# Second layer's modulation on TensorE instead of VectorE, a new hand-over into the down projection, and half of the down weights' low parts on VectorE

## The chip, the cores and the metric

The kernel runs on one core of a Trainium2 chip. The metric is the device time of one execution in microseconds; the time before is the median of three runs. TensorE's clock stands at one of two levels, 1.2 or 2.4 GHz; the profile gives the granted clock as a share of the full one.

## The reference

Two layers over 1024 latent tokens and 256 context tokens of width 1024: layer 0 mixes with a bidirectional RG-LRU, layer 1 with neighbourhood attention, and each is followed by a ConvFFN of width 2816. Each layer is modulated: six rows of 1024 values (shift, scale and gate, twice) come from the conditioning vector and a 1024 x 6144 matrix, once for the latent tokens (`c`) and once for the context tokens (`c_ctx`).

```python
mods = split(silu(c) @ mod_w[l] + mod_b[l], 6)
xl = xl + mods[2] * mixer(modulate(rmsnorm(xl, norm1_g[l]), mods[0], mods[1]))
zl = modulate(rmsnorm(xl, norm2_g[l]), mods[3], mods[4])
xl = xl + mods[5] * conv_ffn(zl, ffn_w_up[l], ffn_conv_w[l], ffn_conv_b[l], ffn_w_down[l])
def conv_ffn(z, w_up, conv_w, conv_b, w_down):
    u = dwconv(z @ w_up, conv_w, conv_b, FFN_CONV // 2)
    g, v = jnp.split(u, 2, axis=-1)
    return (jax.nn.silu(g) * v) @ w_down
```

The context stream needs only the first 16 of layer 1's 48 columns of 128 modulation values, the latent stream all 48.

## The kernel before, in words

All five engine programs are written out by hand: each engine runs its instructions in the order of the code, and semaphores tie them together. Products are made from split operands: a matrix is held as a high part (the value rounded for TensorE, an ACT copy) and a low part (value minus high part, a subtraction), and three matmuls (high x high, high x low, low x high) make one product.

The change lies in the first layer's ConvFFN. `up_first` makes the hidden rows, one pair of columns `i` after another (`KF` = 22 of them), in two rounds each. After the last one its tail still runs inside the next part: ACT's `mid_g`, `mid_v` and `silu`, VectorE's last sum `c21`, the taps `taps_g` and `taps_v`, and `gated`; then SP stores that last row to memory (`store`), and it comes back as the last tile of the next part's moving operand.

`down_first` is that next part. It works in `N` = 132 chunks in three blocks of 44 (blocks 0 and 1: 512 token columns each, block 2: 256). In a block there are four passes of 11 chunks; a chunk is 12 matmuls over two rows of the hidden matrix and two tiles of output. So 88 chunks have 512 columns and 44 have 256. For chunk n SP loads 256 KB of weights (`load_w`, allowed once chunk n - 7 is used, since there are seven pages), ACT makes the high part (`w_high`), and GpSimd, or in block 2 for every fourth chunk VectorE, the low part (`w_low`; `by_dve` decides). In the first pass of each block the moving operand is loaded and split too: `load_h` on SP, `high` on ACT, `low` on VectorE; tile pair x = 10 of block 0 holds the row that `gated` makes last. In ACT's program `high(0, 10)` stands at n = 4, behind `w_high` of chunk 11. In VectorE's program all the `low(0, x)` of block 0 stand ahead of its loop over n, and the `w_low` of chunk n + 7 stands in that loop at n.

Beside this the part makes the second layer's modulation. In 24 steps 1 MB each of `mod_w[1]` are loaded by GpSimd's queue (`load_mod`, two DMAs a step, two buffers). VectorE makes 32 column sums (`columns`, 8 instructions each, every one waiting for the one before), TensorE turns them two at a time (`turn`, 4 transposes behind chunk `TURN_AT`), and VectorE adds the turned columns up (`turned`). TensorE waits in `turn` for `mod_row`, GpSimd in `load_mod` for the sums of step q - 2. From chunk 89 on the next norm runs beside block 2 (`norm.sums`, `root`, `inverse`, `spread`, then `z`), which needs the modulation.

The first layer's modulation is made elsewhere, by `mod_step`: four matmuls with the two conditioning columns stationary, each writing its own 32 partitions of one PSUM bank, and `mod_turn` of four transposes.

Of the kernel before, what the change touches and what calls it, by code (L numbers as in the profile page):

```python
# [2792 lines left out]
def first_places(nc, m):  # L2793

    modring_at, ring_at, z_at, arena = m.at
    page = D * 4
    half = TOK // 2
    row = TOK * 4

    def at(name, place, shape, dt=F32):  # L2800
        return Plan(nc, place).put(name, shape, dt)

    m.f_H = [at(f"f_slotH{p}", ring_at + page * p, [P, BANK], F32R) for p in range(9)]
    m.f_L = [at(f"f_slotL{p}", ring_at + page * p + page // 2, [P, BANK], F32R) for p in range(9)]
# [5 lines left out]
    m.f_mod = [[m.modw.rearrange("p (k n) -> p k n", k=KD)[:, 4 * h:4 * h + 4, :] for h in range(2)],  # L2810
               [at(f"f_mod1{h}", ring_at + page * p, [P, 4, 2 * P]) for h, p in enumerate((5, 8))]]
# [24 lines left out]


def up_first(nc, m, norm, nxt):
# [408 lines left out]
    def vector(dve):  # L3247
# [125 lines left out]
        for i in range(HEAD, KF):  # L3373
# [29 lines left out]
            if more:  # L3403
                low(i + 1, S3)
            else:
                nxt.early_vector(dve)
# [16 lines left out]
def down_first(nc, m, norm, nxt):  # L3423
# [8 lines left out]
    mod_order, mod_row, mod_T, mod_copied = [sem("e_" + n) for n in ("mod_order", "mod_row", "mod_T", "mod_copied")]  # L3432
    part = Bag()
    down = m.t["ffn_w_down"][0].rearrange("(k p) n -> p k n", p=P)
    mod_w = m.t["mod_w"][1].rearrange("(k p) n -> p k n", p=P)
# [6 lines left out]
    MOD_STEPS = 3 * KD  # L3442
    WIDE = 2 * P
    CHAINS = [(q, s) for q in range(KD) for s in range(2)] + [(q, 0) for q in range(KD, MOD_STEPS)]
    TURNS = len(CHAINS) // 2
    PER_PASS = {1: 5, 2: 6, 3: 3, 4: 5, 5: 6, 6: 5}
    CHAIN_AT = [5, 8] + [NX * p + j * NX // n for p, n in PER_PASS.items() for j in range(n)]
    SUM_AT = {at: n for n, at in enumerate(CHAIN_AT)}
    LAST_OF = {q: n for n, (q, s) in enumerate(CHAINS)}
    LOAD_AT = {CHAIN_AT[LAST_OF[q - 2]] + 1: q for q in range(2, MOD_STEPS)}  # L3450
    TURN_AT = {CHAIN_AT[2 * n + 1] + 4: n for n in range(TURNS)}
    assert len(CHAIN_AT) == len(SUM_AT) == len(CHAINS) and len(LOAD_AT) == MOD_STEPS - 2 and len(TURN_AT) == TURNS
    VALUES_AT = max(TURN_AT) + 1
# [9 lines left out]
    def column_sum(n):  # L3463
        return m.zLraw[:, 2 * (n % 4):2 * (n % 4) + 2, BANK:BANK + P]

    def turned_at(n):
        return MISC + n % 2 * BANK
# [34 lines left out]
    def page_free(eng, p):  # L3502
# [3 lines left out]
        else:  # L3506
            eng.wait_ge(mod_row, len(CHAINS))
# [3 lines left out]
    def tiles_free(eng, b, x):  # L3511
# [8 lines left out]
        elif x < 2:  # L3520
            eng.wait_ge(mod_row, len(CHAINS))
# [23 lines left out]
    def load_mod(gp, q):  # L3545
        if q >= 2:
            gp.wait_ge(mod_row, [n for n, (step, s) in enumerate(CHAINS) if step == q - 2][-1] + 1)
        elif q == 0:
            gp.wait_ge(part.prev.g_conv, KF)
        else:  # L3550
            gp.wait_ge(part.prev.prod_done, part.prev.n_products)
        for h in range(2):
            gp.dma_start(m.f_mod[q % 2][h][:, :, :], mod_w[:, 4 * h:4 * h + 4, q * WIDE:(q + 1) * WIDE]).then_inc(mod_in[q % 2], 16)
# [14 lines left out]
    def sync(sp):  # L3568
# [11 lines left out]
        for n in range(PAGES, N):  # L3580
# [34 lines left out]
    def by_dve(n):  # L3615
        return n >= THREE and n % 4 == 1
# [39 lines left out]
    def scalar(act):  # L3656
        prev = part.prev
        for n in range(3, 5):
            w_high(act, n)
        for x in (2, 3):  # L3660
            high(act, 0, x)
        prev.mid_v(KF - 1)
        for n in range(5, 7):
            w_high(act, n)
        for x in (4, 5):
            high(act, 0, x)
        prev.silu(KF - 1)
        for x in range(6, NX - 1):
# [21 lines left out]
    def gpsimd(gp):  # L3690
# [19 lines left out]
    def tensor(pe):  # L3710
        def turn(n):
            pe.wait_ge(mod_row, 2 * n + 2)
            if n >= 2:
                pe.wait_ge(mod_copied, n - 1)
            for b in range(4):
                x = column_sum(2 * n + b // 2)[:, b % 2, :]
                ins = nc.tensor.transpose(ps[:, turned_at(n) + b * P:turned_at(n) + (b + 1) * P], x, m.ident[:, :])
# [3 lines left out]
        for n in range(N):  # L3721
# [40 lines left out]
    def vector(dve):  # L3762
        def turned(n):

            dve.wait_ge(mod_T, n + 1)
            q = CHAINS[2 * n][0]
            src = ps[:, turned_at(n):turned_at(n) + BANK]
            if n < KD:
                nc.vector.tensor_reduce(m.mod[:, 1, :, 2 * q:2 * q + 2], src.rearrange("p (s b x) -> p s b x", s=2, b=2), AX_X, ALU.add).then_inc(mod_copied, 1)
            else:  # L3770
                nc.vector.tensor_reduce(m.mod[:, 1, 0, 2 * q:2 * q + 4], src.rearrange("p (b x) -> p b x", b=4), AX_X, ALU.add).then_inc(mod_copied, 1)

        def columns(n):

            q, c = CHAINS[n]
            if n >= 4 and n % 2 == 0:
                turned(n // 2 - 2)
            dve.wait_ge(mod_in[q % 2], 32 * (q // 2 + 1))
            acc = column_sum(n)
            chain = Order(dve, mod_order, (KD - 1) * n)  # L3780

            def row(k):
                return m.f_mod[q % 2][k // 4][:, k % 4, :].rearrange("p (b n) -> p b n", b=2)

            chain(nc.vector.tensor_scalar(acc, row(0), m.ccol[:, 0, c:c + 1], None, ALU.mult))
            for k in range(1, KD):
                ins = nc.vector.scalar_tensor_tensor(out=acc, in0=row(k), scalar=m.ccol[:, k, c:c + 1], in1=acc, op0=ALU.mult, op1=ALU.add)
                if k < KD - 1:
                    chain(ins)
            ins.then_inc(mod_row, 1)  # L3790

        def mod_values():
            turned(TURNS - 2)
            turned(TURNS - 1)
            dve.wait_ge(mod_copied, TURNS)
            for c, n in enumerate((N_MOD, 2 * KD)):
                nc.vector.tensor_tensor(m.mod[:, 1, c, 0:n], m.mod[:, 1, c, 0:n], vcol(m, "mod_b1", 0, n), ALU.add).then_inc(mod_copied, 1)

        def mod_gains():
            dve.wait_ge(mod_copied, TURNS + 2)  # L3800
# [59 lines left out]
    part.mod_row, part.sums = mod_row, len(CHAINS)  # L3860
# [1110 lines left out]
```

## Time and profile before

| what | us |
|---|---|
| median of three runs | 2914.04 (2911.12 to 2914.94) |
| the profiled execution's own time | 2910.09 |
| its span | 2908.3 |
| down part of the first layer, first product to last | 1160.7 to 1561.0 of the span |
| TensorE busy in the span | 2800.8 (96%) |
| mean granted clock | 0.984 |

Times within the profile are counted from the start of the span. A matmul's record is longer than the distance to the next one, since matmuls overlap, so durations of work on TensorE are read from start to start. "Busy" is the union of the records. An idle time in brackets stands before the instruction, with what released it.

### The profile page before, as it was taken

Reading aid. Unit: us, or ns where it says so; the run is one execution under the profiler, and the core shown is the slowest. Engines: PE = TensorE matmul, PEld = TensorE weight load, DVE = VectorE, ACT = ScalarE, POOL = GpSimd, SP = SyncE. Lnnn points to the kernel's source line nnn. Section 1 sums busy time; section 2 is a strip of 40 time slices with the busy share of each in tenths; the row PEclk is TensorE's granted clock in tenths of the full one; section 3 lists DMA queues with packets and bytes.
Section 4 is the critical chain, followed back from the end, with each engine's and each line's share of the span. In section 5 each row is a group of like instructions: output and inputs, shape, how many; then the busy total and the mean of one; then the engine's idle time right before and its main releaser. Section 6 shows DMA issues by size and latency. Waiting matters only on the chain. (4 is left out here: it accounts for less than half of the span.)

```text
span 2908.3 us, 42045 instructions
## 1 busy us (share of the span) xinstructions
PE 2800.8 (96%) x16269; PEld 2408.3 (83%) x16269; DVE 1892.1 (65%) x2649; ACT 1300.7 (45%) x1881; POOL 821.3 (28%) x639
## 2 busy tenths in 40 slices
PE   8999999999999999888799999999999999999999
PEld 6888887879999999666688888888788788887888
DVE  7667666288888887899955035545638888885111
ACT  6676884164444333323144144444524544444331
POOL 3322230230000000655546343433414000005653
PEclk9999999999999999899899999999999999999999
DMA  9544334211222223756554343332433222227442
GB/s 338 147 120 116 112 89 183 96 33 64 72 71 71 71 71 105 257 175 206 189 192 134 111 142 88 95 88 80 128 124 102 87 87 78 82 68 259 157 132 73
DMA packets 349414, 355.90 MB, mean 122 GB/s; under 512 B 48275, under 2 KB 301554, under 8 KB 347168
## 3 DMA queue, kind: packets, MB, share of 16 engines
q1 hardware_dynamic: 333504, 298.86, 32.4%
q0 software_dynamic: 15680, 54.35, 5.9%
q8 instruction: 131, 2.15, 0.3%
q14 instruction: 67, 0.55, 0.1%
q10 hardware_dynamic: 32, 0.01, 0.0%
HBM read 284.02 MB, written 66.13 MB: 120 GB/s over the span
## 5 line engine op out<-in xcount | busy, mean ns | idle before, releaser
L3624 POOL TENSOR_TENSOR f_slotL<-f_slotS,f_slotH 128x512 fp32r<-128x512 f32 x121 | 167.8, 1404 | 590.3 <-ACT f_slotH L3601 589.9
L4662 POOL TENSOR_TENSOR slotL<-slotS,slotH 128x512 fp32r<-128x512 f32 x88 | 124.2, 1421 | 453.5 <-ACT slotH L4592 453.5
L3210 PE MATMUL ps<-zL,f_slotH 128*128 128x320 f32 x640 | 197.5, 310 | 1.4 <-DVE f_keptR L3268 1.4
L3210 PE MATMUL ps<-zH,f_slotH 128*128 128x320 f32 x640 | 198.1, 310 | 0.5 <-ACT f_snap L3066 0.5
L3210 PE MATMUL ps<-zH,f_slotL 128*128 128x320 f32 x640 | 198.1, 310 | 0.0
L2363 POOL TENSOR_SCALAR S<-S,rowstat 128x608 f32<-128x608 f32 (+1 forms) x63 | 136.0, 2159 | 199.4 <-DVE rowstat L2651 199.4
L3601 ACT ACTIVATE f_slotH<-f_slotS 128x512 fp32r<-128x512 f32 x132 | 81.8, 627 | 220.5 <-DMA f_slotS<-in_ffn_w_down_dram 220.4
L3210 PE MATMUL ps<-f_keptR,f_slotH 128*128 128x320 f32 x640 | 170.1, 310 | 0.0
L2564 ACT ACTIVATE S<-S,rowstat 128x640 f32<-128x640 f32 (+1 forms) x128 | 103.5, 809 | 144.1 <-DVE rowstat L2646 144.1
L4260 PE MATMUL ps<-zH,slotH 128*128 128x512 f32 x400 | 156.2, 391 | 1.2 <-DVE U L4357 1.2
L4260 PE MATMUL ps<-zL,slotH 128*128 128x512 f32 x400 | 156.2, 390 | 1.1 <-DVE slotL L4328 1.1
L4260 PE MATMUL ps<-zH,slotL 128*128 128x512 f32 x400 | 155.8, 390 | 0.0
L2646 DVE CUSTOM_DVE_ANT_0 S<-ps,bias 128x640 f32<-128x640 f32 (+1 forms) x128 | 98.1, 804 | 81.5 <-PE ps L2411 81.0
L776 PE MATMUL ps<-zH,wH 128*128 128x512 f32 (+1 forms) x408 | 145.7, 357 | 0.0
L776 PE MATMUL ps<-zL,wH 128*128 128x512 f32 (+1 forms) x408 | 144.6, 354 | 0.0
L776 PE MATMUL ps<-zH,wL 128*128 128x512 f32 (+1 forms) x408 | 144.6, 354 | 0.0
L4697 PE MATMUL ps<-zH,slotH 128*128 128x512 f32 (+1 forms) x360 | 133.3, 370 | 4.2 <-DVE res_last L4752 2.4
L4697 PE MATMUL ps<-zL,slotH 128*128 128x512 f32 (+1 forms) x360 | 132.4, 368 | 0.0
L4697 PE MATMUL ps<-zH,slotL 128*128 128x512 f32 (+1 forms) x360 | 132.4, 368 | 0.0
L3746 PE MATMUL ps<-zH,f_slotH 128*128 128x512 f32 (+1 forms) x320 | 125.7, 393 | 3.3 <-DVE zL L3612 2.5
L3746 PE MATMUL ps<-zL,f_slotH 128*128 128x512 f32 (+1 forms) x320 | 123.2, 385 | 0.0
L3746 PE MATMUL ps<-zH,f_slotL 128*128 128x512 f32 (+1 forms) x320 | 122.9, 384 | 0.0
(524 smaller groups left out, 8591.2 us busy)
## 6 DMA issues: line engine op xcount, KB each, us to landing
f_slotS<-in_ffn_w_down_dram SPq DMA_DIRECT2D x132, 256.0 KB, 3.3
slotS<-in_ffn_w_down_dram SPq DMA_DIRECT2D x88, 256.0 KB, 2.6
wraw<-in_ffn_w_up_dram SPq DMA_DIRECT2D x36, 512.0 KB, 4.0
modw<-in_mod_w_dram POOLq DMA_DIRECT2D x16, 1024.0 KB, 6.7
wraw<-in_na_w_in_dram SPq DMA_DIRECT2D x32, 512.0 KB, 4.1
bias<-scratch_bias SPq DMA_DIRECT2D x512, 32.0 KB, 1.8
f_slotS<-in_ffn_w_up_dram SPq DMA_DIRECT2D x60, 256.0 KB, 2.9
scratch_h<-f_V SPq DMA_DIRECT2D x22, 640.0 KB, 2.9
```

The source lines that it names most:

```text
L776: last = nc.tensor.matmul(ps[:, slot * SLOT + c:slot * SLOT + c + n], w(k), r(k)[:, c:c + n], start=(k == 0 and i == 0), stop=(k == K - 1 ...
L2363: nc.gpsimd.tensor_scalar(x, x, m.rowstat[:, g % 2, 5:6], None, ALU.mult).then_inc(scaled[1], 1)
L2564: nc.scalar.activation(s, s, ACT.Exp, scale=-1.0, bias=m.rowstat[:, g % 2, hd:hd + 1], accum_out=m.rowstat[:, g % 2, 2 + hd:3 + hd]).then_ ...
L2646: nc.vector.tensor_tensor_reduce(m.S[:, g % 2, hd, 0:n], ps[:, at:at + n], m.bias[:, s % 2, h, hd, 0:n], -1.0, 3.0e38, ALU.add, ALU.min, m ...
L3210: ins = nc.tensor.matmul(out_of(i, p, x), wt[:, w], z, start=(fresh and k == 0 and n == 0), stop=(k == 3 and n == 2), skip_group_check=True)
L3601: nc.scalar.activation(m.f_H[page(n)][:, :], m.f_S[page(n)][:, :], ACT.Copy).then_inc(d_high, 1)
L3624: ops.tensor_tensor(m.f_L[p][:, :], m.f_S[p][:, :], m.f_H[p][:, :].bitcast(F32), ALU.subtract).then_inc(low_dve if by_dve(n) else low_pool, 1)
L3746: ins = nc.tensor.matmul(out, wt, h, start=(x == 0 and kk == 0 and i == 0), stop=(x == NX - 1 and kk == 1 and i == 2), skip_group_check=True)
L4260: ins = nc.tensor.matmul(out, w, z, start=(fresh and k == 0 and n == 0), stop=(k == 3 and n == 2), skip_group_check=True)
L4662: nc.gpsimd.tensor_tensor(m.slotL[slot(n)][:, :], m.slotS[slot(n)][:, :], m.slotH[slot(n)][:, :].bitcast(F32), ALU.subtract).then_inc(d_lo ...
L4697: ins = nc.tensor.matmul(out, wt, h, start=(first and i == 0), stop=(last and i == 2), skip_group_check=True)
```

## The change

It does four things. (1) The modulation of layer 1 is made by TensorE, as in layer 0: 24 steps of four matmuls, step q behind chunk 7 + 3q, three groups of eight steps; each group is copied out by VectorE, turned by four transposes behind the second chunk after it, and added to the bias by VectorE. VectorE's 32 column sums, 16 reductions and TensorE's 16 turns go. (2) The 24 loads of 1 MB move from GpSimd's to SP's queue, in rows of 2048 values instead of 256. (3) The hand-over: in VectorE's program the first two `low` pairs stand behind the last round's `x12`, `c22` and `c12` instead of before them; the later `low`s stand between the taps; ACT's order changes likewise; VectorE clears one PSUM bank. (4) `by_dve` gives VectorE the low part of every second chunk from 7 on.

```diff
@@ up_first, vector, last column @@
-            else:
-                nxt.early_vector(dve)
             x12(i, 1)
             c22(i, 1)
 ...
                 low(i + 1, S4)
+            else:
+                nxt.early_vector(dve)
@@ down_first @@
+    GROUPS, STEPS = N_MOD * P // MODG, N_MOD * P // MODG * KD
+    STEP_AT = [7 + 3 * q for q in range(STEPS)]
+    GROUP_AT = [STEP_AT[KD * g + KD - 1] for g in range(GROUPS)]
@@ load_mod, now called by sync @@
+        if q >= 2:
+            sp.wait_ge(mod_used, q - 1)
 ...
+        g, k = divmod(q, KD)
+        src = mod_w[k][:, g * MODG:(g + 1) * MODG]
+        if q % 2 == 0:
+            sp.dma_start(m.modw[:, :], src).then_inc(mod_in[0], 16)
+            return
+        for h in range(2):
+            sp.dma_start(m.f_mod1[h][:, :], src[:, h * D:(h + 1) * D]).then_inc(mod_in[1], 16)
@@ sync, in the loop over n, behind load_w, store and residual @@
+            for q, at in enumerate([PAGES + 2, PAGES + 4] + [at + PAGES + 1 for at in STEP_AT[:STEPS - 2]]):
+                if n == at:
+                    load_mod(sp, q)
@@ by_dve @@
-        return n >= THREE and n % 4 == 1
+        return n >= PAGES and n % 2 == 1
@@ scalar @@
-        for n in range(3, 5):
-            w_high(act, n)
-        for x in (2, 3):
-            high(act, 0, x)
+        w_high(act, 3)
+        high(act, 0, 2)
+        w_high(act, 4)
+        high(act, 0, 3)
         prev.mid_v(KF - 1)
-        for n in range(5, 7):
-            w_high(act, n)
         for x in (4, 5):
             high(act, 0, x)
         prev.silu(KF - 1)
+        for n in (5, 6):
+            w_high(act, n)
@@ tensor @@
+        def mod_step_of(q):
+            g, k = divmod(q, KD)
+            pe.wait_ge(mod_in[q % 2], (16, 32)[q % 2] * (q // 2 + 1))
 ...
+            for j in range(4):
+                ins = nc.tensor.matmul(ps[32 * j:32 * j + 2, MACC:MACC + BANK], m.ccol[:, k, :], mod_rows(q, j), start=(k == 0), stop=(k == KD - 1))
+            ins.then_inc(mod_used, 1)
 ...
+            if n in STEP_AT:
+                mod_step_of(STEP_AT.index(n))
+            if n - 2 in GROUP_AT:
+                turn(GROUP_AT.index(n - 2))
@@ vector @@
-        for x in (2, 3):
-            low(dve, 0, x)
-        prev.c21(KF - 1, 1)
-        prev.taps_g(KF - 1)
-        prev.taps_v(KF - 1)
-        for x in (4, 5):
-            low(dve, 0, x)
-        prev.gated(KF - 1)
-        for x in range(6, NX - 1):
-            low(dve, 0, x)
-        low(dve, 0, NX - 1)
+        prev.c21(KF - 1, 1)
+        low(dve, 0, 2)
+        prev.taps_g(KF - 1)
+        low(dve, 0, 3)
+        low(dve, 0, 4)
+        prev.taps_v(KF - 1)
+        low(dve, 0, 5)
+        prev.gated(KF - 1)
+        dve.wait_ge(prev.c11_done, 2 * (KF - HEAD))
+        nc.vector.memset(ps[:, MACC:MACC + BANK], 0.0).then_inc(mod_zeroed, 1)
+        for x in range(6, NX):
+            low(dve, 0, x)
 ...
-            if n in SUM_AT:
-                columns(SUM_AT[n])
+            if n - 1 in GROUP_AT:
+                mod_row_of(GROUP_AT.index(n - 1))
+            if n - 3 in GROUP_AT:
+                mod_columns(GROUP_AT.index(n - 3))
```

## Rows read from the trace of the kernel before

**Rows 1.** Windows of the down part: length, busy (x instructions) by engine, clock, DMA.
```profile
1160.74:1191.36 30.62, 24.06 (x84) 18.88 (x85) 23.07 (x31) 16.67 (x27) 14.32 (x9) 0.83 0.71 248
1191.36:1204.96 13.60, 13.60 (x61) 11.26 (x60) 8.02 (x10) 2.94 (x5) 9.15 (x8) 1.00 1.03 372
1204.96:1488.65 283.69, 236.33 (x978) 190.81 (x976) 261.78 (x322) 74.42 (x131) 152.47 (x135) 0.92 0.57 190
1488.65:1561.00 72.35, 69.67 (x565) 67.83 (x563) 50.97 (x62) 41.20 (x73) 50.98 (x37) 1.00 0.66 217
```

**Rows 2.** Waits from 1160 to 1490: who for whom, total, times, longest.
```profile
PE ps L3717 <- DVE zLraw L3787: 47.4, 14, 4.9
POOL modw L3553 <- DVE zLraw L3787: 41.1, 10, 7.6
```

**Rows 3.** Groups by shape from 1160.74 to 1488.65: busy, mean ns, idle before.
```profile
L3624 POOL TENSOR_TENSOR f_slotL<-f_slotS,f_slotH 128x512 fp32r<-128x512 f32 x89 | 121.3, 1380 | 56.7 <-ACT f_slotH L3601 56.3
...
L3787 DVE SCALAR_TENSOR_TENSOR zLraw<-f_mod,ccol,zLraw 128x256 f32<-128x256 f32 x112 | 98.5, 879 | 4.0
L3787 DVE SCALAR_TENSOR_TENSOR zLraw<-modw,ccol,zLraw 128x256 f32<-128x256 f32 x112 | 95.8, 855 | 4.0
```

**Rows 4.** PE's timeline: starts of chunks 0, 7, 60, 61 and 88, one turn.
```profile
1160.74 0.47 PE L3746 MATMUL ps<-zH,f_slotH 128*128 128x512 f32 x1 [0.84 <-issue]
...
1191.36 0.39 PE L3746 MATMUL ps<-zH,f_slotH 128*128 128x512 f32 x1
...
1385.73 1.12 PE L3717 MATMUL ps<-ident,zLraw 128*128 128x128 f32 x4 [4.91 <-DVE zLraw L3787]
1386.50 0.78 PE L3746 MATMUL ps<-f_tH,f_slotH 128*128 128x512 f32 x1
...
1391.45 0.39 PE L3746 MATMUL ps<-zH,f_slotH 128*128 128x512 f32 x1
...
1488.65 0.28 PE L3746 MATMUL ps<-f_mH,f_slotH 128*128 128x256 f32 x1
```

**Rows 5.** PE's timeline in layer 0: a modulation step, later a turn.
```profile
92.60 0.28 PE L1123 MATMUL ps<-xS,wH 96*128 96x256 f32 x1
92.81 1.04 PE L364 MATMUL ps<-modw,ccol 128*2 128x512 f32 x8
93.78 0.50 PE L776 MATMUL ps<-zH,wH 128*128 128x512 f32 x1
94.11 0.40 PE L776 MATMUL ps<-zL,wH 128*128 128x512 f32 x1
...
246.56 0.60 PE L414 MATMUL ps<-ident,modrow 128*128 128x128 f32 x4
```

**Rows 6.** Tile modw, 60 to 400: its loads of 1 MB in rows of 2048 values.
```profile
DMA to landing us min/median/max: 5.0/6.7/9.9
```

**Rows 7.** Hand-over, timeline of DVE (three rows) and ACT (two rows).
```profile
1159.35 2.50 DVE L3612 TENSOR_TENSOR zL<-zLraw,zH 128x512 fp32r<-128x512 f32 x4 [4.20 <-ACT zH L3606]
...
1181.30 1.49 DVE L3339 TENSOR_TENSOR f_V<-f_V,f_G 128x1280 f32<-128x1280 f32 x1
...
1196.06 1.77 DVE L3612 TENSOR_TENSOR f_endL<-f_endS,f_endH 128x512 fp32r<-128x512 f32 x1
...
1163.08 1.46 ACT L3090 ACTIVATE f_G<-f_Ug,vec 128x1280 f32<-128x1280 f32 x1 [2.72 <-DVE f_Ug L3297]
...
1192.62 0.63 ACT L3601 ACTIVATE f_slotH<-f_slotS 128x512 fp32r<-128x512 f32 x1 [5.02 <-DMA f_slotS<-in_ffn_w_down_dram]
```

**Rows 8.** DVE's timeline in block 2.
```profile
1535.76 1.11 DVE L3624 TENSOR_TENSOR f_slotL<-f_slotS,f_slotH 128x512 fp32r<-128x512 f32 x1 [0.60 <-ACT f_slotH L3601]
1536.79 0.73 DVE L723 SCALAR_TENSOR_TENSOR ztmp_t<-res,gain,ps 128x512 f32<-128x512 f32 x1
...
1538.96 1.63 DVE L728 SCALAR_TENSOR_TENSOR zL<-ztmp_t,mod,zH 128x512 fp32r<-128x512 f32 x1
```

**Rows 9.** Windows: the busiest 15 us of block 2.
```profile
1530.00:1545.00 15.00, 15.00 (x124) 14.68 (x123) 13.54 (x17) 10.05 (x19) 14.00 (x10) 1.00 0.76 255
```

More of the change, by code:

```diff
@@ L2809, in first_places @@
     m.f_pages, m.f_page_free = (0, 1, 3, 6, 4, 7, 2), FirstSlots().left
-    m.f_mod = [[m.modw.rearrange("p (k n) -> p k n", k=KD)[:, 4 * h:4 * h + 4, :] for h in range(2)],
-               [at(f"f_mod1{h}", ring_at + page * p, [P, 4, 2 * P]) for h, p in enumerate((5, 8))]]
+    m.f_mod1 = [at(f"f_mod1{h}", ring_at + page * p, [P, D]) for h, p in enumerate((5, 8))]
     m.f_keptR = at("f_keptR", arena, [P, KD, TOK], F32R)
@@ L3431, in down_first @@
     mod_in = [sem(f"e_mod_in{j}") for j in range(2)]
-    mod_order, mod_row, mod_T, mod_copied = [sem("e_" + n) for n in ("mod_order", "mod_row", "mod_T", "mod_copied")]
+    mod_used, mod_zeroed, mod_row, mod_T, mod_copied = [sem("e_" + n) for n in ("mod_used", "mod_zeroed", "mod_row", "mod_T", "mod_copied")]
     part = Bag()
     down = m.t["ffn_w_down"][0].rearrange("(k p) n -> p k n", p=P)
-    mod_w = m.t["mod_w"][1].rearrange("(k p) n -> p k n", p=P)
+    mod_w = m.t["mod_w"][1].rearrange("(k p) n -> k p n", p=P)
     BLOCK = QUADS * NX
@@ L3440, in down_first @@
     PAIR = 2 * P
[L3442 to L3453, printed above, removed]
+    GROUPS, STEPS = N_MOD * P // MODG, N_MOD * P // MODG * KD
+    STEP_AT = [7 + 3 * q for q in range(STEPS)]
+    GROUP_AT = [STEP_AT[KD * g + KD - 1] for g in range(GROUPS)]
     def split3(n):
@@ L3461, in page, with mod_rows @@
         return m.f_pages[n % PAGES]
[L3463 to L3467, printed above, removed]
+    def mod_rows(q, j):
+        if q % 2 == 0:
+            return m.modw[:, j * BANK:(j + 1) * BANK]
+        return m.f_mod1[j // 2][:, j % 2 * BANK:(j % 2 + 1) * BANK]
+    mod_row_at = m.zLraw[:, 0:4, BANK:BANK + P]
     def bank_at(g):
@@ L3543, in load_h, with load_mod @@
             sp.dma_start(tile(RAWS, b, j), m.hD[j][:, at:at + n]).then_inc(hraw_in[x // 2], 16)
-    def load_mod(gp, q):
+    def load_mod(sp, q):
         if q >= 2:
-            gp.wait_ge(mod_row, [n for n, (step, s) in enumerate(CHAINS) if step == q - 2][-1] + 1)
+            sp.wait_ge(mod_used, q - 1)
         elif q == 0:
-            gp.wait_ge(part.prev.g_conv, KF)
+            sp.wait_ge(part.prev.g_conv, KF)
         else:
-            gp.wait_ge(part.prev.prod_done, part.prev.n_products)
+            sp.wait_ge(part.prev.prod_done, part.prev.n_products)
+        g, k = divmod(q, KD)
+        src = mod_w[k][:, g * MODG:(g + 1) * MODG]
+        if q % 2 == 0:
+            sp.dma_start(m.modw[:, :], src).then_inc(mod_in[0], 16)
+            return
         for h in range(2):
-            gp.dma_start(m.f_mod[q % 2][h][:, :, :], mod_w[:, 4 * h:4 * h + 4, q * WIDE:(q + 1) * WIDE]).then_inc(mod_in[q % 2], 16)
+            sp.dma_start(m.f_mod1[h][:, :], src[:, h * D:(h + 1) * D]).then_inc(mod_in[1], 16)
     def early_sync(sp, stage):
@@ L3710, in tensor, with turn @@
     def tensor(pe):
[L3711 to L3714, printed above, removed]
+        def mod_step_of(q):
+            g, k = divmod(q, KD)
+            pe.wait_ge(mod_in[q % 2], (16, 32)[q % 2] * (q // 2 + 1))
+            if q == 0:
+                pe.wait_ge(mod_zeroed, 1)
+            elif k == 0:
+                pe.wait_ge(mod_row, g)
+            for j in range(4):
+                ins = nc.tensor.matmul(ps[32 * j:32 * j + 2, MACC:MACC + BANK], m.ccol[:, k, :], mod_rows(q, j), start=(k == 0), stop=(k == KD - 1))
+            ins.then_inc(mod_used, 1)
+        def turn(g):
+            pe.wait_ge(mod_row, g + 1)
+            if g == 0:
+                prev.all_formed(pe, KF - 1, 0)
+            else:
+                pe.wait_ge(mod_copied, g + 1)
             for b in range(4):
-                x = column_sum(2 * n + b // 2)[:, b % 2, :]
-                ins = nc.tensor.transpose(ps[:, turned_at(n) + b * P:turned_at(n) + (b + 1) * P], x, m.ident[:, :])
+                ins = nc.tensor.transpose(ps[:, MISC + b * P:MISC + (b + 1) * P], mod_row_at[:, b, :], m.ident[:, :])
             ins.then_inc(mod_T, 1)
@@ L3762, in vector, with mod_row_of, mod_columns @@
     def vector(dve):
[L3763 to L3797, printed above, removed]
+        def mod_row_of(g):
+            dve.wait_ge(mod_used, KD * (g + 1))
+            if g > 0:
+                dve.wait_ge(mod_T, g)
+            nc.vector.tensor_copy(mod_row_at, ps[:, MACC:MACC + BANK].rearrange("p (b n) -> p b n", b=4)).then_inc(mod_row, 1)
+        def mod_columns(g):
+            dve.wait_ge(mod_T, g + 1)
+            for s in range(2 if g == 0 else 1):
+                mod_add(nc, m, 1, s, 2 * KD * g).then_inc(mod_copied, 1)
         def mod_gains():
-            dve.wait_ge(mod_copied, TURNS + 2)
+            dve.wait_ge(mod_copied, GROUPS + 1)
             for c in range(2):
@@ L3858, in early_vector @@
             low(dve, 0, x)
-    part.mod_row, part.sums = mod_row, len(CHAINS)
     part.item_added = item_added
```

19 lines of the change are left out of this document (5 added, 14 removed).

## The prediction, made before the change was built or run

> **What bounds the kernel now.** I first cut the down part of the first layer, 400 us of the span, into windows. TensorE is the engine to watch, but it isn't full: in the stretch of chunks 12 to 87 it is busy 236.33 of 283.69 us at a granted clock of 0.92, while VectorE is busy 261.78 [rows 1]. In the stretch just before, chunks 7 to 11, nothing is in the way: 13.60 us for five chunks, 2.72 us a chunk at clock 1.00 [rows 1]. So 76 chunks would take 206.7 us and take 77.0 more. The waits say what is late: TensorE stands 47.4 us, 14 times, at the turns, for VectorE's column sums [rows 2], and that is the whole idle time of the stretch (283.69 - 236.33). The sums are VectorE's bulk, 98.5 + 95.8 us in 224 instructions [rows 3]; GpSimd waits for them too before it loads [rows 2]. The rest of the 77.0 is the turns themselves and the clock: behind a turn waited for 4.91 us, matmuls start 0.43 us apart and chunk 60 takes 4.95 us instead of 2.72, the lower level (1.2 GHz) after an idle TensorE [rows 4]. Block 2 is close to its floor: 44 chunks of 1.44 us (half of 2.72 and a little) are 63 of 72.35 us [rows 1].
>
> **Edit 1, the sums leave VectorE.** VectorE's 224 + 32 instructions and the 16 reductions go, and so do 16 turns. What was late at the turns is then nothing: the new sums come from TensorE itself. The 77.0 us go whole, if nothing takes their place. Nothing else was bound there: GpSimd's low parts waited for ACT, ACT for the loads. -77.0.
>
> **Edit 2, 24 steps on TensorE.** Layer 0 has the same step. The last product before it starts at 92.60 and needs 0.12, the step's eight records (each matmul is two) start at 92.81, the next product at 93.78, and the one after that 0.33 later instead of 0.227 (2.72 / 12) [rows 5]. That is 1.06 + 0.11 = 1.17 us a step, all of it on the path, since TensorE is the bound: 24 x 1.17 = 28.1. Below, 0.97 (93.78 - 92.81): 23.3. Above, at the lower clock level for the first step or two: +2. The three new turns: at most 0.60 each [rows 5], 1.8; their sum must be copied out by VectorE within two chunks and a step, 6.6 us, and ahead of the copy on VectorE stands a `w_low` that waits for a load issued at the same moment. That is about 5 us with the copy, so mostly covered; I put 1 us for three groups (0 to 5).
>
> **Edit 3, loads on SP.** SP issues 36 DMAs more, at some 0.45 us each, 0.6 us a chunk of 2.8: it keeps its lead of seven chunks. GpSimd loses 48 issues. A step's 1 MB is issued one chunk after the step two before, and needed five chunks and a step later, 14.8 us; the same load landed after 5.0 to 9.9 us in layer 0 [rows 6]. The first is issued right behind `store`, and read below. Nothing on the path. What waits behind a late one on SP is weight loads with 7 chunks in hand. 0.
>
> **Edit 4, the hand-over and the first pass.** Before, `c12` stood behind four low instructions (1159.35 to 1161.85), so ACT idled 2.72 us and began `mid_g` at 1163.08; it was free at 1160.36 [rows 7]. Now `c12` goes as soon as its product is there (about 1159), `mid_g` runs at 1160.4, and the first two lows are no later, for they waited for ACT until 1159.35 anyway: TensorE starts at 1160.74 as before [rows 7]. From 1161.9 VectorE then needs 0.5 (`c21`), a wait for ACT's third high until 1163.5, four pairs of lows of 1.2, the taps of 3.3 to 4.3 each, and `gated`, 1.5: it ends at 1177.5 (1176 to 1179) instead of 1182.79 (1181.30 + 1.49) [rows 7], 5.3 us earlier. The lows of chunks 2 to 6 now come close to when TensorE wants them, and it reaches chunk 7 at about 1182 instead of 1191.36.
>
> There it stops, I expect. Chunk 7 is the first of `by_dve`, and its `w_low` stands in VectorE's loop at n = 0, behind all lows of block 0, the last of which needs the row that `gated` has just made: out to memory by `store`, back by `load_h`, through ACT's `high(0, 10)`, which itself stands behind `w_high` of chunk 11 (waiting for its load until 1192.62 [rows 7]). Before, this way ended at 1197.83 (1196.06 + 1.77), 15.0 us after `gated`, and only chunk 10 needed it [rows 7]. Now chunk 7 does. 1177.5 + 15.0, less about 1.5 for fewer GpSimd instructions beside those lows, plus 1.0 for the `w_low` (1.11 in [rows 8]): chunk 7 starts at 1192.0, after some 10 us of idle TensorE, 0.6 later than before. So the first pass gains nothing: +0.6 (1189.5 to 1195, or -1.9 to +3.6). The clock falls in so long a wait; chunk 60 paid 2.2 for it [rows 4], here I take 2.5 (2 to 4). The cover is good for the first modulation load, though, which has 14 us to land. Counted from chunk 7 to 88, 81 chunks: before 297.29 us (1488.65 - 1191.36) [rows 4], at full rate 220.3, which is the same 77.0.
>
> **Edit 5, every second low part on VectorE.** Up to chunk 87 VectorE has room, with 200 us of sums gone: 0. In block 2 it doubles VectorE's part from 11 low parts to 22. In its busiest 15 us VectorE is busy 13.54 and GpSimd 14.00 [rows 9], but VectorE's times are stretched beside GpSimd: the same `z` instruction takes 0.74 to 1.63, and the one that reads PSUM always 0.73 to 0.75 [rows 8]. In two chunks (2.88 us) VectorE would have 0.73 + 0.74 of `z`, 0.7 of low part (an estimate from 1.11 and the 0.74 of the same size) and 0.2 of adds at the short times, 2.4; at stretched ones 0.73 + 1.19 (the middle of 0.74 and 1.63) + 1.11 + 0.2 = 3.2. The slack is seven chunks for weights, and `z` is due only at the end. Between 0 and +6; nearer to the short end, since GpSimd gets 11 instructions fewer: +0.5.
>
> The Trainium skill has a rule on this (SBUF — State Buffer, Who interferes with whom): a VectorE instruction with two SBUF inputs and a GpSimd one that reads SBUF exclude each other for a whole instruction, which speaks against more low parts on VectorE. The trace agrees on who is stretched. By that rule the time held by low parts in block 2 falls all the same (33 x 1.3 us on GpSimd and 11 x 0.7 on VectorE, 50.6, before; 22 of each, 44, after), so the rule would put 0 where I put +0.5.
>
> **The sum.** -77.0 + 28.1 + 1.8 + 1.0 + 0.6 + 2.5 + 0.5 = -42.5. Everything behind the down part starts when it ends, so all of it reaches the end. 2910.09 - 42.5 = 2867.6 in the profiled execution's own measure; the median of the runs is 3.95 above that (2914.04), so 2871.5.
>
> **Rivals.**
> *A, TensorE isn't stopped at chunk 7.* If VectorE's low part of chunk 7 is there when TensorE comes at 1182, 9.4 us of the first pass (1191.36 - 1182) and the clock's 2.5 are gained: -0.6 - 9.4 - 2.5, 2859. For it: nothing else holds chunk 7. Against: an engine's order in the code is its order on the chip.
> *B, the hand-over saves nothing and block 2 is VectorE's.* `gated` ends as late as before (taps stretched beside GpSimd, lows waiting for ACT), +5.3, or `z` and low parts run at their stretched times, 3.2 against 2.88 us for some 20 pairs of chunks, +6, or both: 2877 to 2883. For it: both engines above 90% in [rows 9].
> *C, slower than before: the modulation's loads pace TensorE.* Two buffers, each loaded only after its step. A landing of L us makes two steps take 1.17 + 2.72 + L us; up to L = 14.8 that is hidden. It costs 11 x (L - 14.8) us, so from L = 18.7 on the kernel is slower than before; at L = 20 it is 2871.5 + 57 = 2929. For it: the windows show 372 GB/s and a DMA share of 1.03 where much is loaded at once [rows 1], and the steps ask for 24 MB in 225 us instead of 290, beside the same weights. Against: 9.9 us is the longest landing seen [rows 6], and the mean need, 1 MB and three chunks' 256 KB in 9.33 us, is 190 GB/s, what the stretch moved before.
> *D, the steps don't overlap.* If the four matmuls ran one after another behind these products, eight records of 0.59 would make 4.7 us, +85, 2957. Rows 5 show otherwise.
>
> **Chances.** The forecast 0.75; A 0.10; B 0.12; C 0.02; D 0.01. The forecast's own bounds, from the ends above, are -9 and +10 if all fell together; the cases A and B lie just inside and at the edge. Range 2858 to 2884. A measurement of this kernel can tell about 0.2% (6 us) from no change. Faster 0.96, the same 0.01, slower 0.03 (C and D).
>
> **What would show it.** In the profile after: no waits of TensorE for VectorE's column sums and a granted clock near 1.00 from chunk 12 to 88 (edit 1); 24 steps of eight records, 1.1 to 1.2 us from product to product (edit 2); landings of the 1 MB loads under 14 us (edit 3); `gated` some 5 us earlier, and one wait of about 10 us of TensorE for VectorE's `f_slotL` at chunk 7, at 1182 (edit 4; rival A if it is missing); block 2 as long as before within 2 us (edit 5). Chunk 88 would start near 1446 instead of 1488.65. The prediction is wrong if TensorE waits often in chunks 12 to 87, for whatever.

## The result, and the profile after

| what | before | after |
|---|---|---|
| median of the runs made side by side, us | 2913.05 (2911.12 to 2914.94, 4 runs) | 2866.65 (2865.17 to 2869.81, 4 runs) |
| ratio to before | | 0.984 [0.9825, 0.9859] |
| profiled execution's own time | 2910.09 | 2869.81 |
| its span | 2908.3 | 2868.0 |
| granted clock, mean | 0.984 | 0.992 |

The change makes the kernel 46.4 us faster; 42.5 were forecast, and 2871.5 (2858 to 2884) for the median. The profiled execution after is the slowest of its four, and its down part starts 3.47 us later than before's (1164.21 against 1160.74). That is no work of the change: e1 and e2 below, whose programs are the same up to chunk 7, start this part 3.45 us apart (1164.72 and 1161.27). So the parts are compared below by their lengths.

Windows of the kernel after, core 0: length, then busy time (x instructions) of PE, PEld, DVE, ACT and POOL, granted clock, DMA share, GB/s. The first answers to chunks 0 to 6 in [rows 1], the second and third to chunks 7 to 87 and 12 to 87, the fourth to block 2, the last to [rows 9].

```profile
1164.21:1196.88 32.67, 21.72 (x85) 16.57 (x85) 25.87 (x33) 18.23 (x30) 10.78 (x7) 0.89 0.87 317
1196.88:1448.98 252.10, 252.10 (x1176) 185.56 (x1177) 69.59 (x104) 75.20 (x133) 70.22 (x54) 0.99 0.65 223
1214.56:1448.98 234.42, 234.42 (x1101) 172.98 (x1100) 65.66 (x98) 72.03 (x128) 67.35 (x52) 1.00 0.63 216
1448.98:1521.00 72.02, 69.29 (x565) 67.72 (x563) 48.76 (x72) 41.60 (x73) 33.73 (x26) 1.00 0.67 217
1490.00:1505.00 15.00, 15.00 (x127) 15.00 (x127) 12.74 (x17) 9.62 (x17) 8.58 (x7) 1.00 0.79 261
```

From chunk 7 on TensorE is busy in the whole 252.10 us at a clock of 0.99. Chunks 12 to 87 of these take 234.42 us, all busy and at 1.00; they had taken 283.69, busy 236.33, at 0.92 [rows 1]. VectorE is busy in 69.59 of the 252.10 us. TensorE's waits from 1164 to 1450, all that are left (for whom: total, times, longest):

```profile
PE ps L3753 <- DVE f_slotL L3623: 7.0, 1, 7.0
PE ps L3753 <- DVE f_tL L3611: 2.1, 1, 2.1
PE ps L3753 <- DVE zL L3611: 1.9, 2, 1.6
```

The 47.4 us for column sums [rows 2] are gone; in their place stand 11 us, all in the first pass. PE's timeline (start, length, what; in brackets the idle time before it and its releaser) has the three long ones at chunks 3, 5 and 7, then one step of the modulation and one turn:

```profile
1174.77 0.47 PE L3753 MATMUL ps<-zH,f_slotH 128*128 128x512 f32 x1 [1.62 <-DVE zL L3611]
...
1182.57 0.47 PE L3753 MATMUL ps<-f_tH,f_slotH 128*128 128x512 f32 x1 [2.08 <-DVE f_tL L3611]
...
1196.88 0.80 PE L3753 MATMUL ps<-zH,f_slotH 128*128 128x512 f32 x1 [6.99 <-DVE f_slotL L3623]
...
1266.54 0.39 PE L3753 MATMUL ps<-zH,f_slotL 128*128 128x512 f32 x1
1266.86 1.04 PE L3714 MATMUL ps<-f_mod,ccol 128*2 128x512 f32 x8
1267.83 0.50 PE L3753 MATMUL ps<-zH,f_slotH 128*128 128x512 f32 x1
1268.16 0.40 PE L3753 MATMUL ps<-zL,f_slotH 128*128 128x512 f32 x1
...
1273.40 0.60 PE L3724 MATMUL ps<-ident,zLraw 128*128 128x128 f32 x4
1273.76 0.48 PE L3753 MATMUL ps<-zH,f_slotH 128*128 128x512 f32 x1
```

The step is that of [rows 5]: 0.97 from its start to the next product (1266.86 to 1267.83), and 0.33 from there to the second. Chunk by chunk it costs 1.19: a chunk with a step takes 3.78, the next one 2.85, every other 2.72.

VectorE's timeline says what chunk 7 waited for. It answers to the first three rows of [rows 7]:

```profile
1175.74 5.36 DVE L789 SCALAR_TENSOR_TENSOR f_V<-f_Uv,vec,f_V 128x1023 f32<-128x1023 f32 x4
1181.13 1.29 DVE L3611 TENSOR_TENSOR f_tL<-f_tS,f_tH 128x512 fp32r<-128x512 f32 x2
1182.34 1.48 DVE L3338 TENSOR_TENSOR f_V<-f_V,f_G 128x1280 f32<-128x1280 f32 x1
...
1194.92 0.69 DVE L3611 TENSOR_TENSOR f_tL<-f_tS,f_tH 128x512 fp32r<-128x512 f32 x1 [4.63 <-ACT f_endH L3605]
1195.53 0.69 DVE L3611 TENSOR_TENSOR f_endL<-f_endS,f_endH 128x512 fp32r<-128x512 f32 x1
1196.13 1.29 DVE L3623 TENSOR_TENSOR f_slotL<-f_slotS,f_slotH 128x512 fp32r<-128x512 f32 x2
```

`gated` ends at 1183.82 (1182.34 + 1.48), its row comes back as `f_endS`, and `w_low` of chunk 7, the `f_slotL` at 1196.13, stands behind it in VectorE's order. TensorE starts chunk 7 when it is there.

### The profile page after: what moved, and what is told of

It is laid out like the page before. It is cut to its first block and busy times, and to the rows that moved or that the text cites. A ratio compares the mean times of both kernels' runs of the same rounds, so it can differ in the third digit from the quotient of the medians.

```text
span 2868.0 us, 42040 instructions
## 1 busy us (share of the span) xinstructions
PE 2801.9 (98%) x16409; PEld 2389.9 (83%) x16409; DVE 1694.4 (59%) x2435; ACT 1303.3 (45%) x1881; POOL 710.3 (25%) x539
## 5 line engine op out<-in xcount | busy, mean ns | idle before, releaser
L3623 POOL TENSOR_TENSOR f_slotL<-f_slotS,f_slotH 128x512 fp32r<-128x512 f32 x69 | 93.2, 1353 | 738.5 <-ACT f_slotH L3600 738.4
L3623 DVE TENSOR_TENSOR f_slotL<-f_slotS,f_slotH 128x512 fp32r<-128x512 f32 x63 | 47.4, 755 | 186.3 <-ACT f_slotH L3600 186.1
L3209 PEld LDWEIGHTS ps<-zL,f_slotH 128*128 128x128 f32 x640 | 120.1, 188 | 1.6 <-issue 1.6
```

What stands on the lines that cost most here:

```text
L3209: ins = nc.tensor.matmul(out_of(i, p, x), wt[:, w], z, start=(fresh and k == 0 and n == 0), stop=(k == 3 and n == 2), skip_group_check=True)
L3623: ops.tensor_tensor(m.f_L[p][:, :], m.f_S[p][:, :], m.f_H[p][:, :].bitcast(F32), ALU.subtract).then_inc(low_dve if by_dve(n) else low_pool, 1)
```

## The experiments

Twelve kernels, each timed beside the kernel before on the same chip; its median there was 2913.37 for e1 to e4, 2914.13 for e5 to e8 and 2912.70 for e9 to e12. "From" says which kernel was edited.

| | from | edit | median, us | ratio to before |
|---|---|---|---|---|
| after | | | 2866.65 | 0.9842 [0.9825, 0.9859] |
| e1 | after | VectorE's low parts from chunk 11 | 2857.49 | 0.9803 [0.9787, 0.9820] |
| e2 | after | old split of the low parts | 2857.03 | 0.9805 [0.9791, 0.9820] |
| e3 | after | old split, old hand-over | 2863.62 | 0.9827 [0.9812, 0.9841] |
| e4 | before | the split alone, from chunk 11 | 2888.56 | 0.9915 [0.9900, 0.9929] |
| e5 | after | every step twice (the modulation comes out doubled) | 2888.26 | 0.9911 [0.9894, 0.9927] |
| e6 | after | old hand-over | 2870.73 | 0.9848 [0.9833, 0.9863] |
| e7 | after | lows of chunks 7, 9 before the last `low` | 2858.97 | 0.9809 [0.9794, 0.9823] |
| e8 | before | modulation loads on SP alone | 2886.07 | 0.9904 [0.9889, 0.9919] |
| e9 | e1 | lows of chunks 3 and 5 earlier | 2858.30 | 0.9811 [0.9798, 0.9825] |
| e10 | before | e4 and e8 together | 2906.96 | 0.9977 [0.9968, 0.9986] |
| e11 | e10 | with the new hand-over | 2902.42 | 0.9968 [0.9956, 0.9981] |
| e12 | e9 | steps in pairs | 2853.11 | 0.9796 [0.9782, 0.9809] |

**e1, e2: is the wait at chunk 7 due to the split?**

```diff
 by_dve, e1
-        return n >= PAGES and n % 2 == 1
+        return n >= NX and n % 2 == 1
 by_dve, e2
-        return n >= PAGES and n % 2 == 1
+        return n >= THREE and n % 4 == 1
```

> The changed kernel, with VectorE's low parts from chunk 11 on instead of 7 (7 and 9 back on GpSimd). My theory: the wait of 7.0 us at chunk 7 and the half clock behind it (2.7 us) are made by VectorE's order alone, so 9 to 10 us go: about 2857 us, and TensorE reaches chunk 7 at about 1189 of the span without a wait. Rival: the next thing due in the first pass (the last row of the hidden matrix for chunk 10, or the first 1 MB load for the step behind chunk 7) is as late, and the wait only moves by one to three chunks: 2863 to 2867.

> The changed kernel with the old rule of who makes the low parts (VectorE only every fourth chunk of block 2). My theory: the new split gains nothing between chunks 11 and 131 and costs the wait at chunk 7, so this is as fast as the one with low parts from chunk 11 on, about 2857, within 2 us. Rival: the split relieves GpSimd, which is then late for some chunks: TensorE waits for GpSimd's f_slotL here, and it is slower than the one from chunk 11 on by 3 us or more.

Both are faster than the change by 9.2 and 9.6 us, and equal to each other. TensorE's waits of e1 (1160 to 1450) no longer have an `f_slotL`:

```profile
PE ps L3753 <- DVE zL L3611: 2.5, 4, 1.6
PE ps L3753 <- DVE f_tL L3611: 2.1, 1, 2.1
```

Its chunk 7 starts 25.0 us after chunk 0, instead of 32.7. From chunk 0 to the first product behind block 2 the trace of e1 is 9.2 us shorter than that of the change. So the mechanism is shown: the low parts of chunks 7 and 9, given to VectorE, cost the change 9 us. And as e2 has the old split everywhere and loses nothing, the new split brings nothing once the sums are on TensorE, block 2 included.

**e3, e6: what is the hand-over worth?** The order of `low`, `taps_g`, `taps_v` and `gated`, of ACT's `w_high` and `high`, and the place of `early_vector` go back to the kernel before's; e3 has the old split too.

```diff
 vector, behind up_first
+        for x in (2, 3):
+            low(dve, 0, x)
         prev.c21(KF - 1, 1)
-        low(dve, 0, 2)
         prev.taps_g(KF - 1)
-        low(dve, 0, 3)
-        low(dve, 0, 4)
         prev.taps_v(KF - 1)
-        low(dve, 0, 5)
+        for x in (4, 5):
+            low(dve, 0, x)
         prev.gated(KF - 1)
```

> The kernel before with the new modulation alone: old hand-over, old split of the low parts. My theory: the stretch of chunks 12 to 87 gains all of its 77 us less 28.5 for steps and 1.5 for turns, and the first pass is as before (no wait at chunk 7, old waits at chunks 2 and 4): 2913 - 47 = 2866, the same as the changed kernel within 2 us. Then the other two edits together are worth nothing, and the hand-over is worth what this one lies above the one with the old split and the new hand-over (8 to 10 us). Rival: hand-over or split carry part of the 46 us: 2875 or more.

> The changed kernel with the old hand-over alone (orders of VectorE and ScalarE, early lows ahead of x12). My theory: the wait at chunk 7 hangs on the end of gated, which was 4.3 us later against the start of the part (22.1 to 19.6 us is what the two traces show, 2.5 us), so 2.5 us or somewhat more is lost, 2869 to 2872. Rival: the hand-over has no value while the wait at chunk 7 stands: 2866 to 2868.

With the old split the new hand-over is worth 6.6 us (e2 against e3), with the new split 4.1 (after against e6; the intervals of these two overlap). In the traces chunk 7 starts 5.0 and 2.5 us earlier with it, so 5.0 of the 6.6 and 2.5 of the 4.1 us are shown to lie in the first pass. In e3 it starts 29.96 after chunk 0, and TensorE waits twice:

```profile
PE ps L3753 <- DVE f_tL L3611: 5.6, 1, 5.6
PE ps L3753 <- DVE zL L3611: 2.5, 1, 2.5
```

e3 is also the modulation alone, with its loads on SP: 49.7 us faster than before. The other two edits together took 3.0 of that back, by the medians; the intervals of e3 and the change overlap.

**e5: does a step cost what its records show?**

```diff
+            for twice in range(2):
                 for j in range(4):
-                    ins = nc.tensor.matmul(..., start=(k == 0), stop=(k == KD - 1))
+                    ins = nc.tensor.matmul(..., start=(k == 0 and twice == 0), stop=(k == KD - 1 and twice == 1))
```

> The changed kernel with every modulation step's four matmuls issued twice (the modulation comes out twice as large before its bias). Each doubled step should add what four such matmuls take without the change-over on either side: 0.97 us or less, so +20 to +24 us, 2887 to 2891, if TensorE is the bound and nothing hides them. Rival: TensorE has idle time between chunks that hides them, or the four strips do not overlap when issued back to back: under +10 or over +40.

21.6 us more than the change by the medians, which is 0.90 for each of the 24 sets of four matmuls behind another set. The trace has it finer: a chunk with a doubled step takes 4.64 us instead of 3.78, so such a set costs 0.86. Of the 1.19 of a step that stands alone 0.33 is therefore the change-over from products to a step and back.

**e7: the wait taken away by order alone.** `w_low` of chunks 7 and 9 ahead of the low part of the last tile.

```diff
-        for x in range(6, NX):
+        for x in range(6, NX - 1):
             low(dve, 0, x)
+        for n in (PAGES, PAGES + 2):
+            w_low(dve, nc.vector, n)
+        low(dve, 0, NX - 1)
 ...
-            if n + PAGES < N and by_dve(n + PAGES):
+            if n > 2 and n + PAGES < N and by_dve(n + PAGES):
```

> The changed kernel with VectorE's low parts of chunks 7 and 9 moved ahead of the low pair that needs the last row. My theory: it is the order on VectorE, not who does the work, that makes the wait at chunk 7: it goes, 2857 as with both on GpSimd, within 2 us. Rival: chunk 9's weights land so late that the low of chunk 9 holds up the lows behind it: 2860 or more.

2858.97, close to e1. The wait at chunk 7 shrinks from 7.0 to 2.2 us and chunk 7 starts 26.1 after chunk 0. The two low parts alone, without the stored row ahead of them, cost 1.1 us up to there, and 1.6 more in chunk 7 itself, which takes 5.50 us at a granted clock of 0.69, instead of e1's 3.88.

**e9: the other first waits.** `low(0, 2)` and `low(0, 3)` ahead of `taps_g`, `low(0, 4)` and `low(0, 5)` ahead of `taps_v`.

> The changed kernel with VectorE's low parts from chunk 11 on, and the lows of the first pass each one place earlier among the taps (2, 3, taps_g, 4, 5, taps_v, gated). VectorE's work up to gated is the same in sum, and the waits at chunks 3 and 5 (1.6 and 2.1 us) had it idle in no place, so they go: 2857.5 - 3.7 = 2854. Rival: the later taps hold up silu or the last row, which chunk 10 then waits for: 2857 or more.

Nothing gained. In its PE timeline the waits at chunks 3 and 5 are gone, and one stands at chunk 6, which wants `low(0, 6)`, behind `gated` as before:

```profile
1183.43 0.47 PE L3753 MATMUL ps<-zH,f_slotH 128*128 128x512 f32 x1 [4.04 <-DVE zL L3611]
```

VectorE has a fixed amount to do before chunk 6, and order only chooses which chunk pays: 4.0 in one place, or 4.6 in five.

**e4, e8: what made the old sums slow?** Both leave the sums on VectorE. e4 takes half the low parts from GpSimd, e8 takes the modulation's loads from it.

```diff
 e4, by_dve
-        return n >= THREE and n % 4 == 1
+        return n >= PAGES + 4 and n % 2 == 1
 e8, sync, in the loop over n (and gone from gpsimd)
+            if n in (PAGES + 2, PAGES + 4):
+                load_mod(sp, (n - PAGES - 2) // 2)
+            if n - PAGES - 1 in LOAD_AT:
+                load_mod(sp, LOAD_AT[n - PAGES - 1])
```

> The kernel before with the new split alone (VectorE makes the low parts of odd chunks from 11 on; the column sums stay on VectorE). If VectorE's column sums bound the stretch and the low parts only add to it: 39 low parts of 0.7 to 1.0 us, +27 to +40, so 2940 to 2953. If the sums are stretched by GpSimd's low parts (0.87 us a piece against 0.485 at their shortest), fewer of those give back about half of 85 us: 2895 to 2915.

> The kernel before with its 48 modulation loads issued by SP instead of GpSimd, nothing else. If the column sums are stretched by GpSimd's low parts (a sum of 0.485 us took 5.1 us while GpSimd ran three instructions back to back), the 37 us of issuing were not what stretched them, but GpSimd is less often busy without a gap: -2 to -8 us, 2905 to 2911. Rival: writing the loads' descriptors on GpSimd is what stretches them: -15 to -25, as the new split alone gave. Third: SP now stands in waits for column sums and weights come late: slower than before.

Both missed: 24.8 and 28.1 us faster, each more than half of what the whole change brings. The traces show less of it, chunks 7 to 87 in 278.42 and 273.65 us instead of 297.29, so 18.9 and 23.6; e4's profiled execution is the slowest of its four. The groups of the sums (busy, mean ns of one, idle before), first e4, then e8; before they took 879 and 855 ns [rows 3]:

```profile
L3787 DVE SCALAR_TENSOR_TENSOR zLraw<-f_mod,ccol,zLraw 128x256 f32<-128x256 f32 x112 | 73.5, 656 | 4.0
L3787 DVE SCALAR_TENSOR_TENSOR zLraw<-modw,ccol,zLraw 128x256 f32<-128x256 f32 x112 | 62.3, 556 | 4.0
```

```profile
L3787 DVE SCALAR_TENSOR_TENSOR zLraw<-f_mod,ccol,zLraw 128x256 f32<-128x256 f32 x112 | 84.2, 752 | 4.0
L3787 DVE SCALAR_TENSOR_TENSOR zLraw<-modw,ccol,zLraw 128x256 f32<-128x256 f32 x112 | 84.1, 751 | 4.0
```

Alone a sum takes 0.485 us: 224 would be 109 us. They took 194 before, 136 in e4 and 168 in e8. That is the gain: VectorE was the bound, and in e8 its sums are 26 us shorter and the kernel 28; in e4 they are 58 shorter, VectorE has 31 us of low parts more up to chunk 88 (40 of them), and the kernel is 25 faster. TensorE's waits for the sums fell from 47.4 to 33.4 and 32.1 us.

What stretches a sum is seen where the longest lies. The timelines of the kernel before, GpSimd and then VectorE:

```profile
1242.01 1.61 POOL L3553 DMA_DIRECT2D modw<-in_mod_w_dram  x2 [4.09 <-DVE zLraw L3787]
1243.63 3.79 POOL L3624 TENSOR_TENSOR f_slotL<-f_slotS,f_slotH 128x512 fp32r<-128x512 f32 x3
```

```profile
1242.61 5.11 DVE L3787 SCALAR_TENSOR_TENSOR zLraw<-f_mod,ccol,zLraw 128x256 f32<-128x256 f32 x1
```

The sum begins during GpSimd's two DMA issues and ends at 1247.72, after these and all three low parts queued behind them. In e8 such a run of three low parts costs a sum one of them:

```profile
1229.10 4.17 POOL L3628 TENSOR_TENSOR f_slotL<-f_slotS,f_slotH 128x512 fp32r<-128x512 f32 x3 [3.73 <-ACT f_slotH L3605]
```

```profile
1229.08 1.60 DVE L3787 SCALAR_TENSOR_TENSOR zLraw<-modw,ccol,zLraw 128x256 f32<-128x256 f32 x1
```

All sums of a kernel can be sorted by what GpSimd does meanwhile (counted from the records' overlaps):

| sums of VectorE | before | e8 |
|---|---|---|
| beside nothing of GpSimd | 160, mean 0.485, longest 0.49 | 143, mean 0.485, longest 0.49 |
| beside its computing alone | 35, mean 1.16, longest 1.62 | 81, mean 1.22, longest 1.60 |
| beside a DMA issue of it | 29, mean 2.63, longest 5.11 | none |

The middle row is the rule quoted in the prediction from the Trainium skill (SBUF — State Buffer, Who interferes with whom), which lets each side hold the shared ports for one whole instruction: it agrees, with 1.6 us at the most. The last row goes beyond it: these 29 took 76.2 us, 62 more than at 0.485. The issue alone costs a sum nothing: 11 of the 29 have no low part queued behind the issue, and take 0.49 at most. The other 18 began during an issue with low parts behind it, and each ended 0.3 us after the last low part of that run, after 1.95 to 5.11 us; in e4, 7 sums at an issue with nothing behind it and 6 with low parts behind it show the same. I had counted the issues at their own length alone, and so expected 2 to 8 us of e8. Why a sum that begins during an issue waits for the whole run, and any other for one low part at most, no record shows. e8 also takes GpSimd's waits for the sums away (80.3 us: 41.1 in [rows 2] and 39.2 for `f_mod`), and no run separates these from the issues; but runs of three low parts are there in e8 as well, and hold no sum over 1.60.

**e10, e11: both cures of the old sums together.** e10 is the kernel before with the split (from chunk 11) and the loads on SP; e11 has e9's hand-over too. This asks how much of the gain needed TensorE for the modulation at all.

> The kernel before, sums on VectorE, with the split of low parts from chunk 11 on and the modulation's loads on SP. The two alone gave 24.8 and 28.1 us. If both gains are the same one (GpSimd's bursts no longer stretch the sums), together 30 to 40: 2875 to 2885. If they add up, 2861, and TensorE hardly waits at the turns.

> As the one before, and with the new hand-over in its better order. All but the modulation's place is then as in the best version, so the difference to that one is what moving the sums to TensorE is worth by itself: with 24 steps at 1.19 us against 16 turns at 0.65 and the waits that are left. I expect the first pass to give 5 us more, 2866 to 2878: still slower than the modulation on TensorE. Rival: the sums on VectorE, unstretched, are hidden wholly: 2850 or less, and moving them was not needed.

Missed by far: e10 gains 5.7 us, less than either cure alone, e11 10.3. (The eleven times of e10 lie between 2899.91 and 2910.20 and its interval overlaps e11's, so these two are not told apart.) The sums are the shortest of all kernels (571 and 550 ns), yet the turns are waited for longer than in e4 or e8. The waits of e10, 1190 to 1480 (two rows) and SP's queue, 1205 to 1460 (two rows):

```profile
DVE f_slotL L3628 <- ACT f_slotH L3605: 49.3, 24, 6.3
...
PE ps L3717 <- DVE zLraw L3787: 44.2, 15, 8.7
```

```profile
SPq L3553 <- DVE zLraw L3787: 137.8, 22, 13.9
SPq L3535 <- PE ps L3746: 48.5, 29, 4.1
```

SP stands 137.8 us in `load_mod` for VectorE's sums, and the weights' loads stand behind that; VectorE stands 49.3 us for the high parts of just these weights before it can go on with its sums. In e8 SP stood nearly as long (123.7), but there the weights that came late were GpSimd's business and no sum stood behind them. Each cure is harmless, together they close a ring. No run took this ring alone apart: it is read from the waits.

In the change SP has the same loads, but waits in `load_mod` for a step of TensorE, and from chunk 7 on TensorE waits for nothing.

**e12: the steps in pairs.**

```diff
-    STEP_AT = [7 + 3 * q for q in range(STEPS)]
+    STEP_AT = [10 + 6 * (q // 2) for q in range(STEPS)]
-            if n in STEP_AT:
-                mod_step_of(STEP_AT.index(n))
+            for q, at in enumerate(STEP_AT):
+                if n == at:
+                    mod_step_of(q)
```

> The version with the early lows, its 24 steps issued two together behind every sixth chunk (10, 16, and so on to 76). A step alone costs 1.19 us, one that follows another directly 0.90 (the doubled steps added 21.6 us for 24), so 12 x 0.29 = 3.5 us less: 2850.5. Rival: both buffers are loaded at once and the pair waits for its second load: the gain is lost, 2854 or more.

2853.11, the fastest of all, 13.5 us under the change and 59.6 under before. Its PE timeline around a pair:

```profile
1271.99 0.39 PE L3753 MATMUL ps<-zH,f_slotL 128*128 128x512 f32 x1
1272.31 1.04 PE L3714 MATMUL ps<-modw,ccol 128*2 128x512 f32 x8
1273.16 1.04 PE L3714 MATMUL ps<-f_mod,ccol 128*2 128x512 f32 x8
1274.13 0.50 PE L3753 MATMUL ps<-zH,f_slotH 128*128 128x512 f32 x1
```

A pair costs 2.05 (2.14 from product to product, less the usual 0.227, and 0.13 in the next chunk), where two steps alone cost 2.38. Chunks 7 to 87 take 246.42 us instead of e9's 250.45, 4.0 less; twelve change-overs of 0.33 are 4.0. The ratios of e12 and e9 lie 0.0015 apart and their intervals overlap, so the gain over e9 rests on the stretch more than on the medians.

## Why the prediction was right

**Edits 1 and 2, the sums for the steps: right.** Chunks 7 to 87 took 297.29 us [rows 4] and take 252.10, 45.2 less; -77.0 + 28.1 + 1.8 + 1.0 + 2.5 makes -43.6. Each step measured 1.19 against 1.17, and e5 shows from the other side that steps are paid in full: 0.86 for every set added. Turns weren't waited for at all (1.0 allowed), which is most of the 1.6 between. The prediction took the 77.0 as "the waits and the clock" and that is what went; that it could be had in part without TensorE (e4, e8) it didn't see, since it took the stretching of the sums as given.

**Edit 3, the loads: right.** 1 MB landed after 5.1 to 6.3 us (`modw`) and 4.0 to 8.0 (`f_mod`), inside the 14.8 that the steps leave; no step waited. C and D are out.

**Edit 4, the place right, two sizes wrong.** The wait of TensorE at chunk 7 for VectorE's `f_slotL`, behind the row that `gated` makes, was named, and e1 proves the cause. Chunks 0 to 6 took 32.67 us against 30.62: +2.05 where +0.6 stood. TensorE came to chunk 7 25.7 us after chunk 0 (1196.88 - 6.99 - 1164.21), where 21.3 was expected, and still had to wait. The step that was mis-sized is `gated` "5.3 us earlier". Counted from chunk 0 it ends after 19.6 us instead of 22.05 (1182.79 - 1160.74), so 2.4 earlier. Part of that is `taps_v`, which took 5.36 us beside GpSimd's low parts (4.08 before; 3.3 to 4.3 expected). The way from there to the last low part took 12.4 (1183.82 to 1196.22), 15.0 before, where I had taken 1.5 off. The 19.6, the 12.4 and 0.7 for the `w_low` are the 32.7 measured. And the wait was 7.0 and not 10, since chunks 3 and 5 had already been waited for, which the prediction called "close". For the clock behind the wait 2.5 were set down; chunk 7 took 5.46 us (1196.88 to 1202.34) where a chunk with a step takes 3.78, so 1.7. Chunk 5, behind its wait of 2.1 us, had paid 1.6 already (4.41 us instead of 2.84), which the prediction did not have.

**Rival A was not what happened, but it is what e1 is:** 2857.5 without the wait, and the prediction's price for it was 2859. That the two agree is in part luck: rival A counts 9.4 us gained in the first pass, and e1 gained 5.6 there (25.01 instead of 30.62 up to chunk 7).

**Edit 5: nothing, as expected.** Block 2, from chunk 88 to the first product of the next part, took 75.00 instead of 75.27: -0.3 where +0.5 stood. GpSimd's busy time in the fullest 15 us fell from 14.00 [rows 9] to 8.58, and VectorE's low part takes 735 ns in the mean instead of 1058, `z` 1028 instead of 1119. That is the direction of the rule weighed in the prediction (less time held in all), and as TensorE bounds block 2 it changed no end: e2 has the old split and is as fast.

**The sum.** 45.2 - 2.05 + 0.3 = 43.4 us by parts, 42.5 forecast. That these are only 0.9 apart is partly luck: the stretch gave 1.6 and block 2 0.8 more than forecast, the first pass 1.4 less. The medians say 46.4. The 3 us between are within what single executions of this kernel differ by (after: 2865.17 to 2869.81, and the profiled one is the last), and no part of the trace is named for them. The prediction put the median 3.95 us above the profiled execution; after, it lies 3.2 below, so 2867.6 was forecast for an execution that took 2869.81, and 2871.5 for a median of 2866.65.

Two figures of the prediction are wrong, without changing the forecast. Its own upper ends add up to 2 + 4 + 3.0 + 1.5 + 5.5 = 16 us and not 10, which is beyond the end of its range. And in rival C, 1 MB and three chunks' weights in 9.33 us are 197 GB/s and not 190; 216 were moved in chunks 12 to 87.

What stays open: why a sum that begins during a DMA issue of GpSimd's is held over the whole run of low parts behind it, and whether e10's ring would open with the loads on a third queue, which wasn't tried.

## What to carry to other kernels

When a second job is given to an engine that runs in order, look at what stands in front of it in the first pass, where loads and stores haven't yet their lead: two of VectorE's 63 low parts cost more than all of them brought. Before an engine's slow instructions are moved elsewhere, compare their mean with their shortest: 0.87 against 0.485 us said that a neighbour was the cause, and DMAs issued from another queue than GpSimd's gave more than half of the gain; but two such moves can close a ring of waits, so time each alone and both together. Small sets of matmuls of another shape are paid mostly by the set and partly by the change-over: put those that may be late by some chunks next to each other.

## What the runs showed of the hardware

- A VectorE sum of 0.485 us takes up to 1.6 us beside GpSimd's computing, but up to 5.11 when it begins during a DMA issue of GpSimd's (0.8 us) with computing queued behind it: all 18 such sums of the kernel before ended 0.3 us after the last queued instruction. With nothing queued an issue cost nothing (0.49 at most, 11 sums).
- Four matmuls of two stationary columns, each on 32 partitions of one bank and 512 columns wide, cost 0.86 us as a set behind another set, and 1.19 with the change from and to products of 128 x 128 around them.
- Behind the 7.0 us wait at chunk 7 the first products have records of 0.80 and 0.63 us instead of 0.39, and the granted clock of that chunk is 0.69. A shorter wait can be followed by the lower clock level too: chunk 5, behind 2.1 us, starts with a record of 0.47, but then has 0.63 us ones, a clock of 0.61, and takes 4.41 us; chunk 3, behind 1.6 us, keeps 1.00 and takes 2.84.
